# A two-block diffusion transformer on one core: modulation chunks moved into the attentions, tokens turned straight from their norm, and the experts' ring at the other end of SBUF

## What is computed

```python
def layer_norm(x, g, b):
    xf = x.astype(jnp.float32)
    mu = xf.mean(-1, keepdims=True)
    xc = xf - mu
    var = (xc * xc).mean(-1, keepdims=True)
    return (xc * lax.rsqrt(var + LN_EPS) * g + b).astype(x.dtype)
...
def gqa_attend(q, k, v):
    s = jnp.einsum("bqkgd,bnkd->bkgqn", q, k).astype(jnp.float32) * HEAD_DIM ** -0.5
    p = jax.nn.softmax(s, axis=-1).astype(v.dtype)
    return jnp.einsum("bkgqn,bnkd->bqkgd", p, v)
```

## Time and profile before

| what | value |
| --- | --- |
| median of 3 runs | 3052.48 us (3046.6 to 3057.73) |
| the profiled execution | 3052.42 us, of which the span of the trace 3050.5 us |
| PE busy | 2694.2 us (88%) |
| DVE busy | 1206.7 us (40%) |
| ACT busy | 857.5 us (28%) |
| POOL busy | 183.3 us (6%) |

### The profile page before, as it was taken

How to read it: one execution, slowest core, us unless ns; L and a number is a source line. 1 busy time by engine, 2 the same in 40 slices (tenths; PEclk the granted TensorE clock), 3 DMA queues, 4 the chain that set the end, 5 groups by cost and what they waited for, 6 DMA issues and landing times. The chain is left out here.

```text
span 3050.5 us, 44966 instructions
## 1 busy us (share of the span) xinstructions
PE 2694.2 (88%) x18056; PEld 1899.2 (62%) x18056; DVE 1206.7 (40%) x1954; ACT 857.5 (28%) x1256; POOL 183.3 (6%) x152
## 2 busy tenths in 40 slices
PE   7787699999997699799988959989889989898798
PEld 5666443343342486455444449977569989796698
DVE  3454522211112634422212154468554455345553
ACT  2151111111111223111111134336344354334442
POOL 0001201221003110000000000000100000000000
PEclk9898699999998799799999979999999999899899
DMA  9834799999987434589999955323345344341542
GB/s 369 323 141 183 289 416 426 398 383 411 425 366 315 175 108 187 225 330 417 425 425 424 425 212 207 134 94 138 139 180 205 152 193 165 121 166 49 221 172 76
DMA packets 111756, 778.74 MB, mean 255 GB/s; under 512 B 28088, under 2 KB 29688, under 8 KB 59224
## 3 DMA queue, kind: packets, MB, share of 16 engines
q1 hardware_dynamic: 90472, 717.79, 58.5%
q0 software_dynamic: 12432, 35.75, 3.1%
q10 hardware_dynamic: 8672, 22.71, 1.9%
HBM read 739.41 MB, written 42.61 MB: 256 GB/s over the span
## 5 line engine op out<-in xcount | busy, mean ns | idle before, releaser
L3240 PE MATMUL psum<-second_x_hi,ffn_up_hi 128*128 128x256 f32 x1408 | 401.9, 285 | 22.1 <-DVE ffn_up_lo L3349 22.1
L3240 PE MATMUL psum<-second_x_lo,ffn_up_hi 128*128 128x256 f32 x1408 | 401.3, 285 | 0.0
L3240 PE MATMUL psum<-second_x_hi,ffn_up_lo 128*128 128x256 f32 x1408 | 401.2, 285 | 0.0
L3240 PEld LDWEIGHTS psum<-second_x_hi,ffn_up_hi 128*128 128x128 f32 x1408 | 273.4, 194 | 25.0 <-DVE ffn_up_lo L3349 23.6
L3240 PEld LDWEIGHTS psum<-second_x_lo,ffn_up_hi 128*128 128x128 f32 x1408 | 273.3, 194 | 1.4
L3240 PEld LDWEIGHTS psum<-second_x_hi,ffn_up_lo 128*128 128x128 f32 x1408 | 273.2, 194 | 0.0
L1645 PE MATMUL psum<-experts_ahead_ring_up,experts_ahead_cols 128*64 128x512 f32 x1056 | 235.0, 598 | 0.2 <-issue 0.2
L3317 DVE TENSOR_TENSOR ffn_up_lo<-second_ring_up,ffn_up_hi 128x4096 fp32r<-128x4096 f32 x40 | 177.0, 4426 | 110.1 <-ACT ffn_up_hi L3277 110.1
L1645 PEld LDWEIGHTS psum<-experts_ahead_ring_up,experts_ahead_cols 128*64 128x64 f32 x1056 | 73.6, 137 | 138.0 <-issue 137.2
L2009 DVE TENSOR_TENSOR experts_gated<-experts_silu,psum 128x256 f32<-128x256 f32 (+1 forms) x57 | 21.3, 374 | 313.9 <-ACT experts_silu L1795 313.9
L3277 ACT ACTIVATE ffn_up_hi<-second_ring_up 128x4096 fp32r<-128x4096 f32 x40 | 144.5, 3612 | 1.5 <-DMA second_ring_up<-in_ffn 1.5
(11 more groups left out here) (641 smaller groups left out, 5084.6 us busy)
## 6 DMA issues: line engine op xcount, KB each, us to landing
experts_ahead_ring_up<-in_experts SPq DMA_DIRECT2D x65, 2048.0 KB, 21.8
moe_ring_up<-in_experts SPq DMA_DIRECT2D x65, 2048.0 KB, 23.2
second_ring_up<-in_ffn SPq DMA_DIRECT2D x44, 2048.0 KB, 9.2
experts_ahead_ring_down<-in_experts SPq DMA_DIRECT2D x65, 1024.0 KB, 17.9
moe_ring_down<-in_experts SPq DMA_DIRECT2D x65, 1024.0 KB, 16.1
second_ring_down<-in_ffn SPq DMA_DIRECT2D x44, 1024.0 KB, 5.0
second_ring_up<-in_attn_w_qkv SPq DMA_DIRECT2D x9, 2048.0 KB, 7.7
results<-experts_y ACTq DMA_DIRECT2D x33, 512.0 KB, 11.1
```

What stands on the lines that cost most here:

```text
L3240: last = nc.tensor.matmul(psum[:, 2 * m + kind, 0:LAT], w[:, j, k, at], h[:, k, :], start=k == 0 and which == 0, stop=k == KD - 1 and whic ...
```

## The change

- **Modulation of layer 1.** Chunks 0 to 3 run inside ab_att, after steps 6, 10, 13 and 17, and are turned to columns at its end. Chunks 4 to 11 run inside na_att, after steps 4, 6, 7, 9, 10, 12, 13 and 15, and are stored to DRAM in the transpose stage that follows (na_o). ln1_0 and ln1_1 have no chunks left. The results go to PSUM banks 6 and 7, beside the attention's outputs, so PE waits ahead of a chunk until DVE has scaled the output of unit s-4. DVE adds the bias after each two chunks (`sum_pair`). The same holds for layer 0's second norm: its scale and shift are turned to columns in mod_rest0, beside the ab_in product.
- **ln1_0, h2_0 and the transposes become one stage**, `residual_turn_stage`. PE transposes the normed tokens; ACT drains them in eight 128x128 instructions a tile, with scale and shift of norm and modulation folded into two columns of factors; DVE makes the rows that go to `h_dram` with two operations a tile (folded factors too), and POOL issues the stores. SP meanwhile issues the router's inputs and the ring's first 12 MB, since the ring now lies at the other end of SBUF. The fold of the factors (six 128x1024 operations of DVE and three small ones) is done in ab_out.
- **combine0** now has to apply ln1_0's gain and shift, which x no longer holds: eight more DVE operations of 128x1024 ahead of the first sum, and two more vectors of 512 KB to load.
- **na_o**: SP stores the modulation, waits for it, and loads five vectors, which were loaded in na_att and ln1_1 before.
- **out_product_stage**: `boundary.load` comes ahead of `next_loads`.

```diff
+    def chunk(self, pe, c):
+        pe.wait_ge(self.loaded[c % self.depth], 16 * (c // self.depth + 1))
+        w = self.slots[c % self.depth].rearrange("p (k q n) -> p k q n", k=KD, n=P)
+        to = self.place(c // 4)[:, c % 4 // 2, c % 2, :]
+        for k in range(KD):
+            for q in range(self.tiles):
+                last = self.nc.tensor.matmul(to[q * self.tile:(q + 1) * self.tile, :], self.cs[:, k, :], w[:, k, q, :], start=k == 0, stop=k == KD - 1)
+        last.then_inc(self.products, 1)
...
+    def sum_pair(self, dve, h):
+        dve.wait_ge(self.biases, 16 * self.tiles)
+        dve.wait_ge(self.products, 2 * h + 2)
+        rows = self.rows[:, 2 * h:2 * h + 2, :]
+        self.nc.vector.tensor_tensor(rows, rows, self.place(h // 2)[:, h % 2, :, :], ALU.add).then_inc(self.summed, 1)
...
+                if step in chunk_at:
+                    pe.wait_ge(outs_used, step - 3)
+                    beside.chunk(pe, chunk_at[step])
+            if beside.turn_at is not None:
+                pe.wait_ge(outs_used, n)
+                beside.turn(pe)
...
+                    if u in sum_at:
+                        beside.sum_pair(dve, sum_at[u])
                     nc.vector.tensor_scalar(out(units[u]), psum[:, 6 + u % 2, 0:dh], inv_total[:, u:u + 1], None, ALU.mult).then_inc(outs_used, 1)
+            if beside.turn_at is not None:
+                beside.take_columns(dve)
...
+def folded_rows(nc, dve, chain, vectors, scale_shift, scratch):
+    vec, rows = vectors.buf, scale_shift.buf
+    vectors.wait(dve, 0)
+    vectors.wait(dve, 1)
+    for row in range(2):
+        scale, shift = rows[:, 2 * row, :], rows[:, 2 * row + 1, :]
+        scale_shift.wait(dve, 2 * row)
+        chain.then(nc.vector.scalar_tensor_tensor(scratch, scale, 1.0, vec[:, 1, :], ALU.add, ALU.mult))
+        nc.vector.scalar_tensor_tensor(scale, scale, 1.0, vec[:, 0, :], ALU.add, ALU.mult)
+        scale_shift.wait(dve, 2 * row + 1)
+        chain.then(nc.vector.tensor_tensor(shift, shift, scratch, ALU.add))
...
+def residual_turn_stage(nc, name, psum, ident, x, y, vectors, rows, mod_cols, cols, h_dram, stored, loads):
...
+        @block.tensor
+        def _(pe):
+            for t in range(n):
+                pe.wait_ge(normed, t + 1)
+                for k in range(KD):
+                    last = nc.tensor.transpose(bank(t)[:, k, :], x[:, t, k * P:(k + 1) * P], ident[:])
+                last.then_inc(turned, 1)
+        @block.gpsimd
+        def _(pool):
+            for t in range(n):
+                pool.wait_ge(made, t + 1)
+                nc.gpsimd.dma_start(h_dram[t * P:(t + 1) * P, :], y[:, t, :]).then_inc(stored, 16)
+        @block.scalar
+        def _(act):
+            def columns_of(t):
+                act.wait_ge(turned, t + 1)
+                row = t // 2
+                for k in range(KD):
+                    nc.scalar.activation(cols[:, t, k, :], bank(t)[:, k, :], ACT.Identity, scale=mod_cols[:, KD + k, row:row + 1], bias=mod_cols[:, k, row:row + 1])
+            for t in range(n):
+                act.wait_ge(varied, t + 1)
+                nc.scalar.activation(std[:, t:t + 1], agg[:, t, 1:2], ACT.Sqrt).then_inc(rooted, 1)
+                act.wait_ge(placed, t + 1)
+                nc.scalar.activation(x[:, t, :], x[:, t, :], ACT.Identity, scale=rstd[:, t:t + 1], bias=offset[:, t:t + 1]).then_inc(normed, 1)
+                if t >= 1:
+                    columns_of(t - 1)
+            columns_of(n - 1)
         @block.vector
         def _(dve):
-            for t in range(tok_tiles):
-                vectors.wait(dve, 2 * (t // 2))
-                nc.vector.scalar_tensor_tensor(h[:, t, :], vec[:, 2 * (t // 2), :], 1.0, x[:, t, :], ALU.add, ALU.mult).then_inc(scaled, 1)
-        @block.gpsimd
-        def _(pool):
-            for t in range(tok_tiles):
-                vectors.wait(pool, 2 * (t // 2) + 1)
-                pool.wait_ge(scaled, t + 1)
-                nc.gpsimd.tensor_tensor(h[:, t, :], h[:, t, :], vec[:, 2 * (t // 2) + 1, :], ALU.add).then_inc(shifted, 1)
+            chain = Chain(dve, chain_sem)
+            for step in range(n + 1):
+                if step < n:
+                    t = step
+                    vectors.wait(dve, 2 + t // 2)
+                    chain.then(nc.vector.tensor_tensor(y[:, t, :], y[:, t, :], vec[:, 2 + t // 2, :], ALU.mult))
+                    chain.then(nc.vector.scalar_tensor_tensor(x[:, t, :], x[:, t, :], DN_ALPHA, y[:, t, :], ALU.mult, ALU.add))
+                    nc.vector.bn_stats(stats[:, t, 0, :], x[:, t, 0:BANK])
+                    chain.then(nc.vector.bn_stats(stats[:, t, 1, :], x[:, t, BANK:D]))
+                    chain.then(nc.vector.bn_aggr(agg[:, t, :], stats[:, t, :, :]))
+                    nc.vector.tensor_scalar(agg[:, t, 1:2], agg[:, t, 1:2], EPS, None, ALU.add).then_inc(varied, 1)
+                if step >= 1:
+                    t = step - 1
+                    dve.wait_ge(rooted, t + 1)
+                    chain.then(nc.vector.reciprocal(rstd[:, t:t + 1], std[:, t:t + 1]))
+                    nc.vector.tensor_scalar(offset[:, t:t + 1], agg[:, t, 0:1], rstd[:, t:t + 1], -1.0, ALU.mult, ALU.mult).then_inc(placed, 1)
+            for t in range(n):
+                dve.wait_ge(normed, t + 1)
+                chain.then(nc.vector.tensor_tensor(y[:, t, :], x[:, t, :], rows[:, 2 * (t // 2), :], ALU.mult))
+                nc.vector.tensor_tensor(y[:, t, :], y[:, t, :], rows[:, 2 * (t // 2) + 1, :], ALU.add).then_inc(made, 1)
...
+            for i in (4, 5):
+                vectors.wait(dve, i)
+                for t in range(n):
+                    last = v.tensor_tensor(x[:, t, :], x[:, t, :], vec[:, i, :], ALU.mult if i == 4 else ALU.add)
+                then(last)
...
+            boundary.load(sp)
             next_loads(sp)
-            boundary.load(sp)
...
+                    part = modulation(st2, "mod_rest1", 1, 0, 4, 2, turn_at=0, banks=6)
+                    def tables_and_chunks(sp):
+                        fourier.loads(sp)
+                        part.first_loads(sp)
+                        part.more_loads(sp)
...
-                        loads=fourier.loads, on_pool=fourier.clear)
+                        loads=tables_and_chunks, on_pool=clears, beside=part, chunk_at={6: 0, 10: 1, 13: 2, 17: 3})
...
-            part = modulation(ahead, "mod_rest1", 1, 0, 8, 3, True, later=stream.wbuf)
+            def fold(dve):
+                chain = Chain(dve, fold_chain)
+                folded_columns(nc, dve, chain, mod_cols[:, 2, :, :], ln_cols, ln_loaded)
+                folded_rows(nc, dve, chain, vectors, scale_shift, fold_scratch[:])
             split_rows_product(nc, "ab_out", psum, ident, cols, out_stream, 4, acc, Columns(6, 2, lambda j, t: acc[:, t, j * HEAD:(j + 1) * HEAD], cols),
-                               on_pool=part.clear, first_sync=part.first_loads)
-            rows_of_mod = [mod_dram[0, row, kind * D:(kind + 1) * D] for row in range(2) for kind in (4, 3)]
-            with Stage(nc, "h2_ahead0") as st:
-                scale_shift = Vectors(nc, st, "scale_shift", rows_of_mod)
-                residual_norm_stage(nc, "ln1_0", x, acc, 4, vectors, part)
-                token_rows_stage(nc, "h2_0", x, acc, scale_shift, h_dram, 4, rows_stored)
-    with Stage(nc, "moe0") as moe:
-        routing = Routing(moe, 4, PLANS[0])
-        first_experts(routing)
...
+                def first_loads(sp):
+                    inputs.loads(sp)
+                    ring.kept_loads(sp)
+                residual_turn_stage(nc, "ln1_0", psum, ident, x, acc, vectors, scale_shift.buf, mod_cols[:, 2, :, :], cols, h_dram, rows_stored, first_loads)
+                experts_stage(nc, "experts0", psum, ident, ring, cols, inputs, routing, h_dram, rows_stored, who_dram, results, acc, x, scale_shift.buf)
...
+                        part = modulation(st, "mod_rest2", 1, 4, 8, 1, banks=6, later=stream.wbuf)
+                        part.ahead = part.depth
+                        def next_loads(sp):
+                            part.first_loads(sp)
+                            for c in range(out_stream.depth):
+                                out_stream.load(sp, c)
+                            part.more_loads(sp)
+                        def store_and_rows(sp):
+                            part.store(sp)
+                            vectors.loads(sp)
+                            scale_shift1.loads(sp)
...
+                            beside=part, chunk_at={4: 0, 6: 1, 7: 2, 9: 3, 10: 4, 12: 5, 13: 6, 15: 7})
+                        transpose_stage(nc, "na_o", psum, ident, NA_HEADS, 2, lambda j, t: acc[:, t, j * HEAD:(j + 1) * HEAD],
+                                        lambda engine, j, bank: copy_on(nc, engine, q[:, j, :], bank[:, 0:LAT]), store_and_rows)
+                        rows_product(nc, "na_out", psum, q, out_stream, KD, 2, to_rows(acc))
```

(1 more changed line is left out.)

## The result

The changed kernel took 3100.55 us (median of 4 runs, 3096.64 to 3104.71) against 3052.40 us (4 runs) for the kernel before: ratio 1.0158, 95% interval 1.0136 to 1.0181, slower by 48 us. The profiled execution has a span of 3102.9 us, 52.4 more than the profiled one before; it was the longest of its four runs, 4 us above their median. The prediction was 3065 us, at most 3076: the sign was right, the size was a quarter of the truth.

| stretch | before | after | difference | forecast |
| --- | --- | --- | --- | --- |
| start to ab_att | 154.37 | 156.05 | +1.7 | 0 |
| ab_att | 42.94 | 67.37 | +24.4 | +17.0 |
| Fourier mix, ab_out, to ln1_0 | 70.32 | 73.40 | +3.1 | -1.0 |
| ln1_0 to the router | 60.59 | 43.81 | -16.8 | -25.9 |
| router to the lists' end | 43.59 | 48.64 | +5.1 | -0.5 |

The account below looks back on a forecast made before the run. PE was taken to be full in both attentions. Norm to lists -27.4, first attention +17.0, neighbourhood attention with na_o and ln1_1 +28.1, combine and exits +3.6, boundary -9.0 sum to +12.3 us: 3065 us, range 3043 to 3076.

Parts of the forecast that it names:

- chunk 0 ends at 174.0: +7.5 us: First attention: chunk 0's weight lands at 172.1 us behind the Fourier tables, holding PE's queue; 7.5 of the +17.0 us.
- POOL's issue of the last store and the exit add 1.9: Merged norm stage: DVE ends at 32.6 us, then 1.9 us until the experts start, 26.9 us earlier than before.
- 1.5 back for PE's clock: Layer 0's lists: 1.5 us lost to a lower PE clock, since PE idles while DVE makes the rows.
- The neighbourhood attention, +26.5: na_att: eight chunks at 1.9 us plus 1.0 of waiting (23.2), bias additions 0.8, late transfer ahead of chunk 3 2.5.
- the wait for the scaled output: na_att: PE stands 1.0 us ahead of each chunk until DVE has scaled the output of unit s-4.
- The attentions have no room on PE: Both attentions: PE busy 41.09 of 43.0 us and 36.11 of 38.9 us, so chunks put there cost time.
- the waits are absent: Rival, chance 0.2: the attentions pay only matmuls, additions and the turn, 9.2 and 17.6 us; 3046 us in all.
- combine0, na_o and the boundary: Terms: combine +3 and 0.6 for a stage exit; na_o +2.4; the gains loaded first at the boundary -9.0 us.
- the boundary's 9.0: dil_out: with the gains loaded first, the second tile's L3100 starts at 2832.2 rather than 2841.36 us; -9.0 us.
- The fold in ab_out: ab_out: about 8 us of DVE operations stand where DVE idles 8.16 us for PE; taken as 0.
- The rival on the experts' gaps: Rival, chance 0.1: the earlier ring removes up to 17.4 us of PE's "issue" idle in the experts; 3048 us.
- the rival that the rule supports: Rival, chance 0.05: each of 24 changes between narrow and full tiles drains PE, 8 us in all; 3073 us.

Follow-up runs that it names:

- experiment 1: The changed kernel, but SP issues the first two modulation chunks ahead of the Fourier tables in the first attention; 3093.04 us.
- experiment 2: The changed kernel, but SP stores the merged norm stage's rows instead of POOL, and ACT and DVE wait for their landing in the experts; 3095.59 us.
- experiment 4: The changed kernel, but the ring's first 12.6 MB are issued in the experts stage, as before the change, POOL still storing the rows; 3098.82 us.
- experiment 7: The changed kernel with 48 unread transposes more on PE behind the last tile's in the merged norm stage, POOL's exit kept; 3105.78 us.
- experiment 8: The changed kernel with the ring's loads in the experts stage, rows stored by SP with waits in place of the exit, and 48 unread transposes; 3089.92 us.
- experiment 9: The changed kernel, but chunks 0 to 7 beside the merged norm, 8 to 11 in ln1_1, and the ring's loads in the experts stage; 3051.20 us.
- experiment 5: The changed kernel, but each chunk stands between PE's transposes and output product, in a PSUM bank whose output DVE has long scaled; 3102.49 us.
- experiment 10: The changed kernel with the edits of experiments 1, 2 and 5, na_att's eight chunks issued ahead of na_out's weights, and 48 unread transposes; 3073.35 us.
- experiment 11: Experiment 9 with the first tile's transposes ahead of the fourth chunk, the second bias sum last on DVE, and 32 unread transposes before the router; 3036.42 us.

## Why the prediction was wrong

- **The first attention, "chunk 0 ends at 174.0: +7.5 us".** The step that failed: the chunk was taken to be issued right behind the Fourier tables. SP waits for these to land. The stall was 10.7 us and not some 5, and PE's clock fell to 0.50 in it, so that the chunk took 3.6 us and not 1.9. With the chunks ahead of the wait and the tables half of the stall was gone (experiment 1). A smaller error stood beside it: 167.0 was the landing of the first table; in that same trace the last of the tables' six transfers landed at 169.3 us or later, and SP waits for all six. The line stands in a helper that the diff calls; the order of SP's transfers does not show waits.
- **The norm, "POOL's issue of the last store and the exit add 1.9".** This step failed too. POOL's exit waits until its stores land, 11.0 us behind the ring. Experiments 2 and 4 show it from both sides (SP's stores: 33.2 us to the router; stores with an empty queue: landing 2.9 us). The rest of the term was right: 31.9 us measured, 32.6 forecast.
- **The lists, "1.5 back for PE's clock".** The right mechanism at less than a quarter of its size: 6.6 us on the router alone, and half clock until 380 us. Experiments 7 and 8 settle that it is the clock and not the operands. The idle right ahead of the router is not the whole cause: the clock had been at half since 300 us, in a stage in which PE has little to do, and experiments 7 and 9 show that an idle stretch of 13.5 or 6.5 us brings it down as well. The same behind the stall in na_o: PE idles 3.9 us there, its clock is 0.50 from 1259 to 1265 us, and na_out takes 2.6 us more.
- **The neighbourhood attention, +26.5.** Right in mechanism: the wait for the scaled output 0.88 us (1.0), the fourth chunk's weight late by 4.3 us, and its own run at half clock 1.7 us more, which had no term. Measured +30.1. Experiments 5 and 10 take the two waits away one after the other.
- **The attentions have no room on PE.** Right, and it decides the sign: with every wait gone the chunks still cost 16.4 us in na_att. The rival "the waits are absent" gave 3046 us, 6 below the kernel before; experiment 10, where most are gone, is 20 above it. There ab_att still has 16.4 us more than before (4.3 of them a wait for the first chunk), the lists 7.5 more for DVE's wait for the stores, and combine0 and the Fourier mix with ab_out 10 more, of which the sum had 2.6.
- **combine0, na_o and the boundary** came within 1.1 us of their terms; the boundary's 9.0 left out DVE's own product between ACT's squares and L3192. The fold in ab_out cost nothing: DVE still idled 0.86 us behind it.
- **The rival on the experts' gaps** was wrong: the "issue" time ahead of the down products is 19.1 us, where it was 17.4.
- **The Trainium skill** ("TensorEngine Tiling (Array Packing)", Key Properties) says that changing the tiling mode drains the engine. In experiment 5 a chunk costs 2.08 us where its records last 1.95 and PE's next instruction begins 1.88 us behind its start: this leaves at most 0.2 us for its two changes, 2.4 us for all 24. Whether the engine drains is not shown; the rival that the rule supports had 8 us for it, and that is out.
- **Open:** the Fourier mix and ab_out took 3.1 us more than before, where 1.0 less was forecast. It is not the stall in the first attention: they take 71.9 us in experiment 1, where half of it is gone, and as much in experiments 4 and 7, where all of it is there. The experts' main part took 3.8 us more than before. In the other kernels it lies between 574.3 and 580.6 us with no clear order by the ring's start; its cause was not found, nor that of +1.7 us ahead of the first attention, which is within the scatter between kernels (153.9 to 157.0 us).

## What to carry to other kernels

Work moved from a stage that waits for transfers into one whose engine is full costs all of its time, however well it is placed: eight chunks 16.4 us in the neighbourhood attention. Beside the merged norm eight chunks are not free either (46.11 and 47.23 us with them in experiments 9 and 11, 36.06 without in experiment 4, thus 10 to 11 us, set by the landing of their weights), but the other four cost less than 1 us in ln1_1, and that version is the fastest. A queue's list must be read with its waits, and with those of helpers: ask for each moved transfer what the issuing engine stands in just ahead of it, and for each stage's end what it lets the engines finish. And a stall on PE, or a stage in which it has little to do, is dearer than its length: count what PE does next at half clock.

## What the runs showed of the hardware

- A stage's exit waits for transfers that POOL issued in it (11.0 us with 12.6 MB ahead in the changed kernel, 3.3 us with none in experiment 4), and not for those that SP issued (2.5 us from the start of DVE's last row to the router in experiment 2, with stores landing 13.3 us after issue).
- PE idle for 6.5 us (experiment 9) and 13.5 us (experiment 7) ahead of the router, with the granted clock at 1.00 before, was followed by 64 matmuls wholly at 0.50 (1.2 GHz), 13.9 us. After 7.5 us (experiment 2), 10.4 us (experiment 4) and 18.1 us (the changed kernel) it was the same, but there the clock had been at 0.50 in the stage before, too. Behind 1.4 to 1.7 us of idle and a busy stretch the same matmuls ran at full clock (2.4 GHz), 7.3 us.
- Transposes that nobody reads raised the clock from 0.50 to 1.00 in experiments 7, 8 and 11. They help when they reach up to the work that needs the clock, and give nothing when 13.5 us of idle follow.
